# Recurrence: the products that build a unit's transfers and values, taken from the two row halves by turns

## What is computed

```
def step(S, inp):
    w_t, k_t, v_t, kk_t, a_t = inp[:5]
    sa = jnp.einsum('bhvk,bhk->bhv', S, -kk_t)
    S = (S * w_t[:, :, None, :] + sa[..., None] * (kk_t * a_t)[:, :, None, :]
         + v_t[..., None] * k_t[:, :, None, :])
    y = jnp.einsum('bhvk,bhk->bhv', S, inp[5]) if len(inp) == 6 else None
    return S, y
```

## Time and profile before

| | us |
|---|---|
| median of 3 runs | 4187.14 |
| lowest, highest | 4180.54, 4193.31 |
| the profiled execution: its own time | 4180.58 |
| its span, first to last instruction | 4178.2 |
| PE busy | 3711.2 (89%) |
| granted PE clock, mean | 0.942 |
| first scores of unit 0 to last outer products of unit 15 | 2814 to 3674 |

### The profile page before, as it was taken

The page is one execution under the profiler, slowest core; times in us unless marked ns, Lnnn a source line. Parts: engine busy times, 40 slices in busy tenths (PEclk is TensorE's granted clock), DMA queues, the critical chain, the costliest instruction groups (busy, mean ns, idle before and its releaser), DMA issues.

```text
span 4178.2 us, 80819 instructions
## 1 busy us (share of the span) xinstructions
PE 3711.2 (89%) x35670; PEld 2623.3 (63%) x35670; DVE 1542.8 (37%) x2712; ACT 926.6 (22%) x1484; POOL 910.3 (22%) x662
## 2 busy tenths in 40 slices
PE   8897799878877989989999989859999999988997
PEld 3354455533324567658888855438888888846885
DVE  3246421221124655423333440204445555523333
ACT  2032011111112134322111121312233232203221
POOL 0002100011111000013223220025454444404441
PEclk9997899979989999999999989979999999989999
DMA  4207044159970100021111113420000000011221
GB/s 167 91 31 306 11 162 170 72 212 357 369 280 26 41 11 1 27 95 51 61 61 68 74 51 123 170 90 4 14 13 14 14 13 14 3 56 59 108 101 41
DMA packets 64585, 379.12 MB, mean 91 GB/s; under 512 B 12906, under 2 KB 12906, under 8 KB 26352
## 3 DMA queue, kind: packets, MB, share of 16 engines
q1 hardware_dynamic: 40032, 291.52, 17.9%
q0 software_dynamic: 20608, 68.82, 4.2%
q10 hardware_dynamic: 3600, 13.63, 0.9%
HBM read 380.21 MB, written 44.04 MB: 102 GB/s over the span
## 4 chain that ended last, share of the span: by engine, by line
PE 78%; DVE 6%; DMA 5%; POOL 4%; ACT 3%; issue 2%; SPq 0%; DVEq 0%; ACTq 0%; POOLq 0%
PE psum L449 31%; PE psum L461 7%; PE psum L462 7%; PE psum L463 7%; PE psum L619 4%; DMA arena<-in_wall 3%; PE psum L1866 2%; PE psum L2595 2%; PE psum L497 2%; PE psum L2582 2%; PE psum L537 2%; PE psum L638 2%; PE psum L1893 1%; PE psum L2884 1%; PE psum L2560 1%
## 5 line engine op out<-in xcount | busy, mean ns | idle before, releaser
L449 PE MATMUL psum<-arena,ring 128*128 128x512 f32 (+2 forms) x2176 | 797.9, 527 | 15.3 <-DVEq L3661 7.6
L449 PE MATMUL psum<-arena 64*64 64x64 f32 (+4 forms) x14024 | 645.8, 237 | 48.5 <-POOL arena L2818 22.9
L449 PEld LDWEIGHTS psum<-arena,ring 128*128 128x128 f32 (+1 forms) x2176 | 410.5, 189 | 401.0 <-issue 367.3
L449 PEld LDWEIGHTS psum<-arena 64*64 64x64 f32 (+2 forms) x14024 | 519.7, 141 | 142.6 <-issue 105.5
L477 POOL TENSOR_TENSOR ring_low<-ring,slab_high 128x2048 fp32r<-128x2048 f32 x66 | 304.0, 4620 | 1260.0 <-ACT slab_high L470 1259.9
L461 PE MATMUL psum<-h_high,slab_high 128*128 128x512 f32 (+1 forms) x1056 | 377.7, 358 | 23.1 <-DVE h_low L2251 16.7
L462 PE MATMUL psum<-h_low,slab_high 128*128 128x512 f32 (+1 forms) x1056 | 376.0, 356 | 0.0
L463 PE MATMUL psum<-h_high,ring_low 128*128 128x512 f32 (+1 forms) x1056 | 375.7, 356 | 0.0
L461 PEld LDWEIGHTS psum<-h_high,slab_high 128*128 128x128 f32 x1056 | 200.9, 190 | 56.9 <-issue 15.0
L1866 PE MATMUL psum<-arena 128*64 128x512 f32 x768 | 189.5, 648 | 36.8 <-DMA arena<-in_wall 35.2
L463 PEld LDWEIGHTS psum<-h_high,ring_low 128*128 128x128 f32 x1056 | 201.1, 190 | 28.4
(11 more groups left out here) (341 smaller groups left out, 4826.3 us busy)
## 6 DMA issues: line engine op xcount, KB each, us to landing
ring<-in_wall SPq DMA_DIRECT2D x181, 1024.0 KB, 5.0
arena<-in_wall SPq DMA_DIRECT2D x96, 1024.0 KB, 12.1
moe_rows<-arena POOLq DMA_DIRECT2D x2, 6144.0 KB, 61.2
arena<-moe_rows ACTq DMA_DIRECT2D x24, 512.0 KB, 8.4
moe_out<-arena POOLq DMA_DIRECT2D x24, 512.0 KB, 8.9
arena<-spill POOLq DMA_DIRECT2D x8, 1024.0 KB, 5.0
spill<-arena POOLq DMA_DIRECT2D x2, 3072.0 KB, 17.6
filters<-arena POOLq DMA_DIRECT2D x2, 2048.0 KB, 6.6
```

The source lines that it names most:

```text
L449: last = L.eng.matmul(out, a, b, start=(i == 0), stop=(i == len(pairs) - 1))
```

## The change

`feats_tensor` takes both row halves and both kinds of product in one call. It claims all four banks first (in the same ring order: p = 0 both kinds, p = 1 both kinds) and waits until all four are free. Then, for each kind, it goes through the tiles, and in each tile through p = 0 and p = 1, so that two banks are filled together, one from each row half. A bank's bank_full is raised with its own last product, in the last tile. DVE's program is unchanged, and so is every product, operand and place of a result.

```diff
-def feats_tensor(L, p, pairs, n=TT):
-
-    ps = L.next_bank()
-    for bank_free, count in L.bank_frees:
-        L.eng.wait_ge(bank_free, count)
-    for tt in range(n):
-        for hh in range(2):
-            last = matmuls(L, ps[64 * hh:64 * hh + 64, tt * CH:(tt + 1) * CH], pairs(hh, tt, p))
-    last.then_inc(L.bank_full, 1)
+def feats_tensor(L, products, n=TT):
+
+    banks = []
+    for p in range(2):
+        for pairs in products:
+            banks.append((L.next_bank(), L.bank_full))
+            for bank_free, count in L.bank_frees:
+                L.eng.wait_ge(bank_free, count)
+    for i, pairs in enumerate(products):
+        for tt in range(n):
+            for p in range(2):
+                ps, bank_full = banks[len(products) * p + i]
+                for hh in range(2):
+                    last = matmuls(L, ps[64 * hh:64 * hh + 64, tt * CH:(tt + 1) * CH], pairs(hh, tt, p))
+                if tt == n - 1:
+                    last.then_inc(bank_full, 1)
...
-    for p in range(2):
-        feats_tensor(L, p, lambda *at: [(square(B.ua, *at), tok(B.betok, *at))])
-        feats_tensor(L, p, lambda *at: [(tok(B.betok, *at), square(B.uv, *at)), (tok(B.katok, *at), tok(B.vtok, *at))])
+    feats_tensor(L, (lambda *at: [(square(B.ua, *at), tok(B.betok, *at))],
+                     lambda *at: [(tok(B.betok, *at), square(B.uv, *at)), (tok(B.katok, *at), tok(B.vtok, *at))]))
...
-    for p in range(2):
-        feats_tensor(L, p, lambda *at: [(square(B.ua, *at), square(B.rbt, *at))], TX)
-        feats_tensor(L, p, lambda *at: [(square(B.uv, *at), square(B.rbt, *at)), (tok(B.vtok, *at), square(B.rkt, *at))], TX)
+    feats_tensor(L, (lambda *at: [(square(B.ua, *at), square(B.rbt, *at))],
+                     lambda *at: [(square(B.uv, *at), square(B.rbt, *at)), (tok(B.vtok, *at), square(B.rkt, *at))]), TX)
```

## The result

The changed kernel takes **4216.15 us** (median of 11 runs, 4200.01 to 4232.94), the kernel before beside it 4187.14 (11 runs, 4166.03 to 4227.51). The ratio is 1.0066, 95% interval 1.0039 to 1.0094: slower by over 0.3%, and outside the predicted range. The profiled execution took 4215.96 us (span 4213.5), against 4180.58.

A forecast was written before the change was run, and what follows sets the result against it. PE's outer products and DVE's reads behind them were taken to bound ten unit ends, POOL's operand six. A gain of 18.5 us less 5.4 for the clock gave 13.1 us, a median of 4174 us, range 4162 to 4197.

The forecast's parts named there:

- PE's pace: Outer products at unit ends: four quadrants side by side, 14.8 ns a record, 240 records in 3.55 us, not 6.64.
- first rival: Outer products at a pace between, some 4 us less, 4183; by a 25 ns floor, 4185.6; chance 0.28.
- DVE's reads: Unit ends: DVE reads banks 0.34 to 0.54 us apart, last read at 4.86 in place of 6.90, 2.04 us less.
- What reaches the end: Of 16 unit ends, eight gain in full (16.3 us), two 1.1 us each, six nothing: 18.5 us.
- Waits for banks: Each outer-product call at a unit end waits for four banks at once; costed at nothing.
- The clock: Idle PE at six POOL-bound unit ends: low clock behind four, 1.36 us each, 5.4 us lost; bound 16 us.
- last rival: Unit ends: six idle times each cost twice the clock price, 16 of 18.5 us gone, 4185; chance 0.12.
- slower rival: Outer products: alternating halves no faster than one half, last read 0.92 us later; 13 us slower, 4200; chance 0.10.

The follow-up runs named there:

- e1: Changed kernel with every outer product made four times in the alternating order: 4548.65 us, one run.
- e3: Changed kernel with two unneeded 512-column products in TensorE's wait for POOL at even unit ends: 4198.26 us, ratio 1.0040 to the kernel before.
- e4: Kernel before with three of four tiles of the output products left out, 36 of a unit's 120 products: 4233.86 us, ratio 1.0129.
- e5: Changed kernel with unneeded products at even and odd unit ends and the inversion's third level: 4168.99 us, ratio 0.9958 to the kernel before.
- e9: Kernel before with one unneeded 512-column product per unit at the inversion's third level: 4167.04 us, ratio 0.9962.

## Why the prediction was wrong

By its steps:

1. **PE's pace**: right in kind. In a burst it is 15.3 to 16.6 ns a record, forecast 14.8, and under the 25 ns from which the first rival's 4185.6 was worked out. But I applied it to all 240 records, and in e1 TensorE gets its instructions no faster than 256 in 3.5 to 4.0 us. That rate, 27 to 31 ns a record, is all but what the old order uses; a faster order lives on what is already loaded. The first rival, the pace between, asked whether PE can be fed faster for 240 records. It can't in any of the changed kernel's 16 ends (only unit 4 of e3, whose borders fell outside, shows it), and the question was worth more than its 0.28, though it priced the effect as a pace in between, not as a stop of 1 us.
2. **DVE's reads**: right. In the end of e3 without a pause inside, the reads start at 2.37, 2.84 and so on to 4.76 us, forecast 2.28, 2.82 to 4.86. With the pause inside, the last one comes at 5.93.
3. **What reaches the end**: 18.5 us forecast, 13.4 at full clock by the fit, 11 by the clocks of all runs. Mis-sized: with the pauses the last read gains 0.97 us, not 2.04.
4. **Waits for banks**: all but right. The first outer product waits 0.84 to 1.01 us in place of 0.78, 1.4 us over the 16 ends. One pause, the 1.8 us of unit 2, is put down by the profile to a read of DVE (L3136), but its first waiting instruction is at 193 of its block like the others: it is the block's border, which there falls on the second call.
5. **The clock**: this is the step that failed. The price was about right: 1.36 us for a stretch of 3.4 us is 0.40 for each us, against 0.38 and 0.40 in the fits and 0.35 over all runs. From a single pair of stretches that is partly luck. The number and length were wrong. I counted one short stretch behind each of four POOL waits, and bounded it by six at twice the price, 16 us. The trace has 15 stretches in place of 6, nine of them of 13.7 or 17.1 us, 116 us more: 157 x 0.38 - 41 x 0.40 = 43 us, where I had 5.4. The last rival, the clock takes it back, had the mechanism and a third of its size (16 us).

Sum by the measured terms: 43.3 - 13.4 = 29.9 us, measured 30.3 in the recurrence. The price and the full-clock lengths come from fits that use these two kernels too, so this sum shows that the two terms suffice, not more; that low clock is the cause rests on e4, e5 and e9, and on the clocks of all runs.

The slower rival, banks filled together that end together, is not what happened: the last read comes earlier at every end, not 0.92 us later. The kernel is slower for a reason that I had on the wrong side of zero.

What the row should have told me: that a stretch with TensorE two thirds busy is followed by low clock already in the kernel before, which has 41 us of it. Every microsecond taken from TensorE's work without taking it from the unit's length is idle time, and I treated the present clock as given.

The change is not useless: with its idle time filled it takes 4168.99 us. But 16 fillers in the levels of the kernel before give 4167.04 (ratio 0.9962, 0.9945 to 0.9979), with nothing alternating. That is the version to keep. The two stood in different groups of runs; that they are equal is all that can be said. Open are whether and why the odd ends need their filler in the changed kernel, and whether the other microsecond could be had by spreading the outer products' instructions, so that two borders lie further apart in time; the second was not tried.

## What to carry to other kernels

Before making a burst of small products faster, compare its pace with the rate at which the engine's instructions arrive, and see in the trace how many records run before the first stop that is released by "issue". Before removing work or time from TensorE at a place where it then waits for another engine, look at the granted clock around it: if there is low clock already, price the edit by all the stretches that the new idle time may bring, and test it with unneeded products put into waits that exist. Such a filler is itself an edit worth trying, if it lies wholly inside a wait: here one of 512 columns in a wait of 1.15 us, once in a unit, gave 0.4%.

## What was not expected of the hardware

TensorE's instruction blocks: 128 pairs of weight load and matmul in 2.15 us, then 1.3 to 1.8 us of standing, again and again (e1). The largest surprise is e4, with 30% of the outer products left out and 55 us slower: 283 us of the recurrence at 0.50, against 41. And one 1.1-us product per unit (e9), 16 in a recurrence of 800 us, takes the low clock from 41 to 7 us.
